# First query weights of the attention split inside the state-space units; the first job begins before its stage; rotations one job behind

## The reference

```python
q, k, v, z, xbc, dt_raw, gates = jnp.split(h @ w_in, IN_SPLITS, axis=-1)
q = apply_rope(q.reshape(nb, ns, 8, 2, 64), cos, sin)        # u*cos + rot(u)*sin
k = apply_rope(k.reshape(nb, ns, 8, 2, 64), cos, sin)
k_all = concatenate([hc @ w_k, k]); v_all = concatenate([hc @ w_v, v])
...
y_lat = yf + rev(yb) + d * xh                                # chunked state-space scan
y = y_lat * silu(z)
yg = yg * rsqrt(mean(yg * yg) + EPS)                         # by group of 256 channels
y = (yg * g_ssd_norm)
```

## Time and profile before

| | us |
|---|---|
| median of three runs | 3079.74 |
| lowest, highest | 3074.94, 3081.43 |
| span of the profiled execution | 3080.3 |
| TensorE busy in it | 2933.2 (95%) |
| DVE, ACT, POOL busy | 1776.7, 1435.4, 538.9 |

### The profile page before, as it was taken

One profiled execution on the slowest core, in us unless ns is written; L12 is line 12 of the kernel. 1 busy time (PEld: TensorE's weight loads), 2 busy tenths in 40 slices (PEclk: granted clock), 3 DMA queues, 4 the chain that ended last, 5 costly groups with the idle time before them and its releaser, 6 DMA issues. The chain is left out here.

```text
span 3080.3 us, 38613 instructions
## 1 busy us (share of the span) xinstructions
PE 2933.2 (95%) x15514; PEld 2375.0 (77%) x15514; DVE 1776.7 (58%) x1996; ACT 1435.4 (47%) x1913; POOL 538.9 (17%) x626
## 2 busy tenths in 40 slices
PE   8999999898999999999999899999999998899998
PEld 4878888786887578777777478788888896688887
DVE  4448755546644788888888264555544326455543
ACT  3345525437223478888787133533333325443332
POOL 0016513224101633323222100000001002000000
PEclk9999999999999999999999999999999998899999
DMA  5220111021762599999999551233332310233331
GB/s 206 55 64 1 45 46 56 28 56 59 229 196 87 205 336 371 362 370 373 372 380 355 219 197 47 55 97 96 103 103 69 113 39 32 76 89 96 96 101 44
DMA packets 278385, 456.07 MB, mean 148 GB/s; under 512 B 24864, under 2 KB 206752, under 8 KB 258112
## 3 DMA queue, kind: packets, MB, share of 16 engines
q1 hardware_dynamic: 251712, 398.82, 37.5%
q0 software_dynamic: 26496, 54.79, 4.9%
HBM read 451.16 MB, written 39.08 MB: 159 GB/s over the span
## 5 line engine op out<-in xcount | busy, mean ns | idle before, releaser
L264 DVE TENSOR_TENSOR weight_part<-weights,weight_part 128x2048 fp32r<-128x2048 f32 (+1 forms) x62 | 140.6, 2267 | 157.0 <-ACT weight_part L253 157.0
L1193 ACT ACTIVATE up_conv<-banks,tap_columns 128x512 f32<-128x512 f32 x88 | 68.5, 778 | 292.4 <-PE banks L311 292.4
L253 ACT ACTIVATE weight_part<-weights 128x2048 fp32r<-128x2048 f32 (+1 forms) x62 | 116.0, 1871 | 172.7 <-PE banks L306 167.2
L781 POOL TENSOR_SCALAR branch_mean<-branch_mean 128x1 f32<-128x1 f32 x20 | 10.4, 521 | 1059.0 <-ACT up_conv L775 713.3
L1237 DVE SCALAR_TENSOR_TENSOR up_conv<-banks,tap_columns,up_conv 128x511 f32<-128x511 f32 x88 | 65.9, 749 | 218.0 <-ACT up_conv L1193 218.0
L306 PE MATMUL banks<-hT_r,weight_part 128*128 128x512 f32 x448 | 176.5, 394 | 0.3 <-PEq L3857 0.3
L311 PE MATMUL banks<-hT_r,weight_part 128*128 128x512 f32 x448 | 175.6, 392 | 0.0
L264 DVE TENSOR_TENSOR weight_part_o<-weights,weight_part_o 128x2048 fp32r<-128x2048 f32 (+2 forms) x46 | 100.0, 2175 | 117.8 <-ACT weight_part_o L253 117.8
L3310 POOL DMA_INDIRECT gathered<-h_tokens,block_rows x64 | 115.6, 1806 | 203.6 <-PE banks L3427 189.1
L306 PE MATMUL banks<-hT_r,weight_part_o 128*128 128x512 f32 x384 | 151.0, 393 | 0.0
L311 PE MATMUL banks<-hT_r,weight_part_o 128*128 128x512 f32 x384 | 150.2, 391 | 0.0
(11 more groups left out here) (728 smaller groups left out, 8888.6 us busy)
## 6 DMA issues: line engine op xcount, KB each, us to landing
weights<-in_w_e_gate SPq DMA_DIRECT2D x44, 1024.0 KB, 15.6
weights<-in_w_e_up SPq DMA_DIRECT2D x44, 1024.0 KB, 18.2
hT<-in_w_e_down SPq DMA_DIRECT2D x44, 1024.0 KB, 18.6
weights<-in_w_up SPq DMA_DIRECT2D x88, 512.0 KB, 5.2
gate_up<-in_w_e_gate SPq DMA_DIRECT2D x22, 1024.0 KB, 15.6
gate_up<-in_w_e_up SPq DMA_DIRECT2D x22, 1024.0 KB, 18.3
down<-in_w_e_down SPq DMA_DIRECT2D x22, 1024.0 KB, 18.3
weights<-in_w_down SPq DMA_DIRECT2D x20, 1024.0 KB, 5.0
```

What stands on the lines that cost most here:

```text
L253: c.nc.scalar.activation(self.pair(n)[0][:, 0:z], self.raw[n % RAW_SLOTS][:, 0:z], ACT.Copy).then_inc(self.high_ready, 1)
L264: c.nc.vector.tensor_tensor(low[:, 0:z], self.raw[n % RAW_SLOTS][:, 0:z], high[:, 0:z].bitcast(F32), ALU.subtract).then_inc(self.low_ready, 1)
L1193: nc.scalar.activation(a[:, f % 2, v], c.ps[:, 2 * (f % 4) + v], ACT.Identity, scale=conv[:, 2, ch:ch + 1], bias=bias[:, ch:ch + 1]).then_ ...
```

## The change

- The state-space units' block: SP starts the transfers of the two query and two key tiles behind those of `z`. In unit 13 ACT and DVE split the first query tile, into the memory of `c.x`, which the third `z` tile has used. In place of the 14 filler products TensorE waits for unit 14's SiLU and issues five steps of the first query work.
- `plain_transpose` becomes `gain_transpose`: it uses banks 4 to 7; TensorE issues no filler, but 3, 2 and 4 steps of the two first works behind the transposes of tiles 1, 2 and 3. ACT splits the second query tile behind tile 1, DVE behind tile 2, into a pair of buffers at `KEYS_AT`, where keys and values come to lie later.
- `project_heads`: the first half gets its first job with one step left for each of its two works. Where a first job is opened so, in both halves, its works release no rotation; rotations wait in a list, and each later work ends with the oldest. `high_made` and `low_made` become counts.

```diff
@@ SplitRing
-    def ahead(self, sp, tiles, pairs=()):
+    def ahead(self, sp, tiles, pairs=(), back=2):
...
-            self.borrowed[first + i] = (pair, first - 2)
+            self.borrowed[first + i] = (pair, first - back)
...
     def high_ahead(self, c, act):
-        if self.lent is None:
+        if self.lent is None and len(self.sizes) and self.highs not in self.borrowed:
             self.buffers(c, None)
+        made, self.high_made = self.high_made, 0
         self.high(c, act)
-        self.high_made = True
+        self.high_made = made + 1
@@ gain_transpose (was plain_transpose; its filler and its transfers are gone)
+        def bank(t, k):
+            return c.ps[:, 4 + 2 * (t % 2) + k // 4, (k % 4) * P:(k % 4 + 1) * P]
...
                 last.then_inc(taken_a, 1)
+                if t == 1:
+                    c.split.high_ahead(c, act)
...
                 last.then_inc(taken_v, 1)
+                if t == 2:
+                    c.split.low_ahead(c, dve)
...
-            warm(c, 7, 24)
+                for v, k in steps[t]:
+                    opened.step(c, v, k)
@@ project_heads
-            pending = None
+            pending = []
...
-                    if pending is not None:
-                        rotate(pending)
-                        pending = None
+                    if pending and not (opened and n == 0):
+                        rotate(pending.pop(0))
                     if w["rope"]:
-                        pending = r
+                        pending.append(r)
...
-            if pending is not None:
-                rotate(pending)
+            for later in pending:
+                rotate(later)
@@ block1_mixer
+        opened = Opened(h)
+        steps = [(v, k) for v in range(2) for k in range(KD - 1)]
+        q_and_k = [[(KD, FT2, cols(w_in, c0 + n * FT2, FT2))] for c0 in (Q0, K0) for n in range(2)]
+        x_parts = c.rounded(c.x)[:].rearrange("p t d -> p (t d)")
...
+            keys_at = c.over(xt, "second_tile", [P, 2, PART], F32R, KEYS_AT)
+            pairs = [[x_parts[:, i * PART:(i + 1) * PART] for i in range(2)], [keys_at[:, i] for i in range(2)]]
...
+                    q_and_k, pairs, opened, steps[0:5])
...
+                           opened, [(), steps[5:8], steps[8:10], steps[10:]])
@@ ssd, last block
             c.split.load(sp, z_tiles(w_in))
+            c.split.ahead(sp, following, pairs, 1)
...
             pe.wait_ge(ready, U - 1)
-            warm(c, 3, 14)
+            pe.wait_ge(silud, U - 1)
+            opened.take(c, pe)
+            for v, k in steps:
+                opened.step(c, v, k)
...
+                if i == U - 3:
+                    c.split.high_ahead(c, act)
...
+                if i == U - 3:
+                    c.split.low_ahead(c, dve)
@@ diff_attention
-  pool_work=part_keys, tables=(tables, landed, 32, rot_r[:], rot[:]) if hh == 0 else None, opened=opened[0] if hh else None)
+  pool_work=part_keys, tables=(tables, landed, 32, rot_r[:], rot[:]) if hh == 0 else None, opened=opened[0] if hh else begun)
```

More of the change, by code:

```diff
@@ L174, in __init__ @@
         self.kept, self.settled, self.lent = None, False, None
-        self.high_made = self.low_made = False
+        self.high_made = self.low_made = 0
     def buffers(self, c, s, spare=()):
@@ L224, in high_ahead @@
     def high_ahead(self, c, act):
-        if self.lent is None:
+        if self.lent is None and len(self.sizes) and self.highs not in self.borrowed:
             self.buffers(c, None)
+        made, self.high_made = self.high_made, 0
         self.high(c, act)
-        self.high_made = True
+        self.high_made = made + 1
     def low_ahead(self, c, dve):
+        made, self.low_made = self.low_made, 0
         self.low(c, dve)
-        self.low_made = True
+        self.low_made = made + 1
     def settle(self, ins):
@@ L240, in high @@
         if self.high_made:
-            self.high_made = False
+            self.high_made -= 1
             return
@@ L256, in low @@
         if self.low_made:
-            self.low_made = False
+            self.low_made -= 1
             return
@@ L350, in step, with gain_transpose @@
         return mm3(c, c.ps[:, v], [x[:, at:at + P] for x in self.slot], [x[:, k] for x in self.h], k == 0, k == KD - 1)
[L353 to L358, removed]
+def gain_transpose(c, src, nt, nk, dst, gain, opened, steps):
     nc = c.nc
     with ExitStack() as s:
-        turned = c.sem("pt_turned")
-        taken_v = c.sem("pt_taken_v")
-        taken_a = c.sem("pt_taken_a")
+        turned = c.sem("gt_turned")
+        taken_v = c.sem("gt_taken_v")
+        taken_a = c.sem("gt_taken_a")
         block = s.enter_context(nc.Block())
[L367 to L370, removed]
+        def bank(t, k):
+            return c.ps[:, 4 + 2 * (t % 2) + k // 4, (k % 4) * P:(k % 4 + 1) * P]
         @block.scalar
@@ L376, in _ @@
                 for k in range(4, nk):
-                    last = nc.scalar.activation(dst(k, t), turned_block(c, t, k, None), ACT.Copy, scale=gain(k) if gain else 1.0)
+                    last = nc.scalar.activation(dst(k, t), bank(t, k), ACT.Copy, scale=gain(k))
                 last.then_inc(taken_a, 1)
+                if t == 1:
+                    c.split.high_ahead(c, act)
         @block.vector
@@ L384, in _ @@
                 for k in range(4):
[L385 to L388, removed]
+                    last = nc.vector.tensor_scalar(dst(k, t), bank(t, k), gain(k), None, ALU.mult)
                 last.then_inc(taken_v, 1)
+                if t == 2:
+                    c.split.low_ahead(c, dve)
         @block.tensor
@@ L397, in _ @@
                 for k in range(nk):
-                    b = 2 * (t % 2) + k // 4
-                    last = nc.tensor.transpose(c.ps[:, b, (k % 4) * P:(k % 4 + 1) * P], src(t)[:, k * P:(k + 1) * P],
-                                               c.ident[:])
+                    last = nc.tensor.transpose(bank(t, k), src(t)[:, k * P:(k + 1) * P], c.ident[:])
                     if k in (3, nk - 1):
                         last.then_inc(turned, 1)
-            warm(c, 7, 24)
+                for v, k in steps[t]:
+                    opened.step(c, v, k)
 NEG = -1e30
@@ L1802, in block1_mixer @@
         yT = c.sb(s1, "yT", [P, KD, SEQ])
+        opened = Opened(h)
+        steps = [(v, k) for v in range(2) for k in range(KD - 1)]
+        q_and_k = [[(KD, FT2, cols(w_in, c0 + n * FT2, FT2))] for c0 in (Q0, K0) for n in range(2)]
+        x_parts = c.rounded(c.x)[:].rearrange("p t d -> p (t d)")
         with ExitStack() as s:
             xt = c.sb(s, "x_ssd", [P, TC, D])
+            keys_at = c.over(xt, "second_tile", [P, 2, PART], F32R, KEYS_AT)
+            pairs = [[x_parts[:, i * PART:(i + 1) * PART] for i in range(2)], [keys_at[:, i] for i in range(2)]]
             with ExitStack() as st:
-                ssd(c, st, w_in, h, hc, xt, yT, lambda *room: front(c, h, hc, low, lowc, lam, cond, subln, ssd_gain, yT, xt, *room))
-            plain_transpose(c, lambda tile: xt[:, NC + tile], NT, KD, lambda k, tile: yT[:, k, tile * P:(tile + 1) * P], lambda k: ssd_gain[:, k:k + 1],
-                            ahead=[[(KD, FT2, cols(w_in, c0 + n * FT2, FT2))] for c0 in (Q0, K0) for n in range(2)])
+                ssd(c, st, w_in, h, hc, xt, yT, lambda *room: front(c, h, hc, low, lowc, lam, cond, subln, ssd_gain, yT, xt, *room),
+                    q_and_k, pairs, opened, steps[0:5])
+            gain_transpose(c, lambda tile: xt[:, NC + tile], NT, KD, lambda k, tile: yT[:, k, tile * P:(tile + 1) * P], lambda k: ssd_gain[:, k:k + 1],
+                           opened, [(), steps[5:8], steps[8:10], steps[10:]])
         oT, o_low = c.sb(s1, "oT", [P, KD, SEQ]), c.sb(s1, "oT_low", [P, KD, SEQ])
@@ L1811, in block1_mixer @@
         o_parts = (c.rounded(oT), c.rounded(o_low))
-        opened = diff_attention(c, w_in, h, hc, lam, o_low, o_parts, subln, hc_flat)
+        opened = diff_attention(c, w_in, h, hc, lam, o_low, o_parts, subln, hc_flat, opened, keys_at)
         c.clear_sems()
@@ L2080, in _, with ssd @@
             nc.vector.tensor_scalar(lam[:], lam[:], -LAM_INIT, None, ALU.add)
-def ssd(c, s0, w_in, h, hc, xt, yT, first):
+def ssd(c, s0, w_in, h, hc, xt, yT, first, following, pairs, opened, steps):
     nc, t = c.nc, c.t
@@ L2565, in _, with diff_attention @@
                     nc.vector.tensor_copy(tokens(j, 0, 4), c.ps[:, 4 + 2 * (j % 2)].rearrange("p (t n) -> p t n", n=P)).then_inc(taken_v, 1)
-def diff_attention(c, w_in, h, hc, lam, o_low, o_parts, gcol, hc_flat):
+KEYS_AT = 46 * 256
+def diff_attention(c, w_in, h, hc, lam, o_low, o_parts, gcol, hc_flat, begun, second_tile):
     nc, t = c.nc, c.t
@@ L2589, in diff_attention @@
                     v = c.sb(sh, "v", [P, TC, GW])
+                    if hh == 0:
+                        at = c.placed[id(second_tile)][2]
+                        assert c.placed[id(kT)][2] <= at and at + 8 * PART <= c.placed[id(v)][2] + 4 * TC * GW
```

## The result

The changed kernel takes 3062.0 us (median of 8 runs, 3057.24 to 3071.02), the kernel before 3079.84 beside it (8 runs, 3072.72 to 3084.52). The ratio is 0.9943, with a 95% interval of 0.9932 to 0.9955: 17.6 us faster, between 14 and 21. On another chip, in 6 runs beside 17 of the kernel before, it was 0.9946 (0.9932 to 0.9960), 16.6 us. The forecast was 15.3 us less.

What follows compares the result with a forecast made beforehand. TensorE, busy 2933.2 of 3080.3 us, was taken as the bound, so only its idle, slow or filler time counted. Gains of 14.86 and 0.57 less 0.10 made 15.3, taking 3079.74 to 3064.4 us, range 3058.5 to 3071.0.

Steps and rivals of the forecast that it cites:

- The tail: After the last unit's diagonal products: five real steps replace 14 fillers, so the transposes start later; cost 0.24 us.
- The transposing block: 32 transposes with nine steps (27 products) among them replace filler; ends at 383.90 us, against 383.19 with filler.
- the cover: In the transposing block, the second tile's splits and tile 3's copies finish by 382.4, before TensorE's end; margin 1.5 us.
- The stage starts at once: Start of the attention's first half: split waits and idle 4.62 us vanish, third work begins at 385.64; gain 14.86 us.
- rotations are only postponed: First half of the attention: rotations come later, two matrix products each as before.
- Unit 13: Splitting the first query tile in this state-space unit costs 0.1 us; bounds 0 and 4.2 if cover failed.
- SP and the rotation matrix: Early weight transfers clear the queue; the matrix lands at 388.7 us, before the first rotation at 391.24; price 0.
- The lag: Projections of both halves: later rotations make nothing wait, margins 0.6 to 3.4 us; cost 0, up to 2 per half.
- The second half: Start of the attention's second half: the third work needs only the low part; gain 0.57 us, bounds 0 and 1.1.
- the one of the clock among the transposes: Rival: clock falls in the transposing block, its 27 products and six behind run slower; 6.2 us, total 3070.6; chance 0.06.
- the hand-offs: Rival: late rotation matrix stalls the first rotation 1.8 us and thin margins fail; about 3 us, total 3067.5; chance 0.08.
- the slower one: Rival: DVE's finish sets TensorE's pace in sixteen rotated works, 2.0 us each, 32 in all; total 3096; chance 0.02.

Runs made afterwards that it cites:

- the lag alone: Only the list that postpones rotations by one more work, added to the kernel before; ratio 0.9980 (0.9969 to 0.9991).
- the run again: The changed kernel unchanged, measured once more for scatter beside the other experiments on their chip; ratio 0.9946 to the kernel before (0.9932 to 0.9960).

## Why the prediction was right

It said 3064.4, with 3058.5 to 3071.0; it was 3062.0. In the code that was edited the mechanism was right and the sizes too. By its own points:

1. *The tail.* Forecast: transposes 0.24 later than before. The last of the 15 products starts at 374.37 and ends at 374.77; transposes start 4.05 us into the stretch, against 3.73. Cost 0.32. Right.
2. *The transposing block.* Forecast 373.59 to 383.90, 10.31, to the end of its last product; measured 375.07 to 385.01, 9.94. The six changes between kinds of work, taken at 0.05 each, cost less than that together with the ends. ACT's and DVE's splits lay beside the products; the run without the early steps shows that DVE would have ended the block only 0.5 sooner, not 1.4, so the cover, 1.5 in the working, was thinner than it said.
3. *The stage starts at once.* Forecast gain 14.86, measured 15.1; no stall, no low clock. Its sentence that rotations are only postponed left out what else the lag does there (point 6). The filler's share of it was shown from both sides (3.5 to be had by leaving it out before, 5.3 and 5.4 to be paid for putting it in), and so was that of the early steps (11.0 when they are missing).
4. *Unit 13.* ACT splits at 350.69 and DVE at 354.47, and the exponentials of the units before and behind keep their distance, 7.46 and 7.47:

```profile
349.77 1.02 ACT L2399 ACTIVATE dt_a_masked_o<-banks 128x1024 f32<-128x1024 f32 x1 [1.12 <-PE banks L2361]
350.69 1.91 ACT L255 ACTIVATE x_tok_r<-weights 128x2048 fp32r<-128x2048 f32 x1
357.23 1.02 ACT L2399 ACTIVATE dt_a_masked_o<-banks 128x1024 f32<-128x1024 f32 x1 [1.12 <-PE banks L2361]
364.70 1.02 ACT L2399 ACTIVATE dt_a_masked_o<-banks 128x1024 f32<-128x1024 f32 x1 [1.12 <-PE banks L2361]
```

   Cost 0 where 0.1 was taken.
5. *SP and the rotation matrix.* DVE rounds it at 389.15, 3.5 us behind its issue at 385.67, as in the earlier trace rows with an empty queue. The first rotation came 3.2 us later and did not wait. Right.
6. *The lag.* No wait of TensorE in the rest of the first half's projections. Right, but its worth was missed: the gain of point 3 needs the lag, and without it 3.3 us of that gain are lost to a wait for the rotation matrix and `raw_low`.
7. *The second half.* Forecast gain 0.57. The lag itself gains 0.59 where the level rises 3 us into the half (the lag alone; the run again has 49.86 us to the last rotation, 0.58 less than before). In the changed kernel's first profile 1.31 were lost instead, because the level rose only 8.5 us into the half; with the level low so long the lag gains 0.4. The forecast had the work right and no term for how long the level stays low, which differs between executions of one kernel.

Of the rivals, the one of the clock among the transposes did not come, the hand-offs did not bind, and the slower one found nothing: from the third work on, no wait of TensorE shows until the score products. What the prediction had no term for is the share of low clock elsewhere. The edited code gains 15.1 + 0.6 = 15.7 us at best and 13.8 in the first pair of profiles; the timed gains of 17.6 (14 to 21) and 16.6 us take in both. So the last 2 us need no cause of their own, and none is shown. But the agreement is in part luck. On the chip of the run again, the mean clock over the runs is 0.9862 for the changed kernel and 0.9836 for the one before: 42.4 against 50.4 us of missing full rate, 8 us less, of which the edited stretch explains 1.7 (half of the 3.4 us that before spent at half rate there). Span times mean clock falls by only 9.2, less than the edited code saves. Where the other gain in clock and the loss of work lie, no run shows; in the first pair of profiles 5.9 us gained and 4.3 lost in untouched stages stand against each other.

## What to carry to other kernels

Filler at the end of a block costs its full time where the next stage's inputs are ready (5.3 us for 48 instructions), and most of it where they get ready only behind the block's end (3.5 of 5.5 us). Where real steps of the next stage can stand in its place, they are work that would have to be done anyway (here 42 products of 0.233 us for 8.9 us of filler), and the level held. Before a job is cut down to its last steps, look at what was hidden behind it: here a table of 64 KB and a rounding that the old, long job had covered, and which would have taken 3.3 us back without the lag. When an edit moves work out of a stretch, count to an instruction behind which both kernels have done the same: the way to the fourth work made 1.06 us out of a gain of 0.59. When two profiles differ by more than the edited stretch shows, compare the start of the same instruction stage by stage with the granted clock beside it, before looking for a further effect of the edit.

## What the hardware showed that I had not expected

Two kernels with the same instructions in the same order at the start of the second half had the granted clock low to 8.5 us and to 3.2 us into it (changed kernel, 12.39 us; run again, 10.49 us). A block of 32 transposes between waits of 3.57 and 4.28 us ran at a clock of 0.71, and one with the same transposes and 27 products among them at 1.00; in the first the level rose while TensorE did only transposes. In the attention of the second block the same work took 94.9, 93.6 and 89.0 us at clocks of 0.86, 0.87 and 0.92, the last two in two executions of one kernel that reach it within 0.8 us of each other. That is up to 6 us, a third of this change, from one untouched stage of one profile.
